# A feed-forward whose seven products run block by block, with sums chained in PSUM

## The reference, cut to what matters

```python
D_FF = 2816
def swiglu(h, w_in, w_out):
    g, u = jnp.split(h @ w_in, 2, axis=-1)
    return (jax.nn.silu(g) * u) @ w_out
# in the first block, after the mixers (x: 1024 x 1024, float32):
x = layer_norm(ALPHA * x + g1 * y, ln1_w, ln1_b)
x = layer_norm(ALPHA * x + g2 * swiglu(x * (1.0 + sc2) + sh2, w_ffn_in, w_ffn_out), ln2_w, ln2_b)
```

## Time and profile before

| | us |
|---|---|
| median of 3 runs | 2177.39 (2175.89 to 2180.31) |
| profiled execution, its own time | 2175.72 |
| its span | 2173.9 |
| feed-forward, first matmul to last | 606.84 to 1313.05 |
| next stage's first matmul | 1329.03 |

### The profile page before, as it was taken

One profiled execution on the slowest core, in us unless ns is written; L12 is line 12 of the kernel. 1 busy time (PEld: TensorE's weight loads), 2 busy tenths in 40 slices (PEclk: granted clock), 3 DMA queues, 4 the chain that ended last, 5 costly groups with the idle time before them and its releaser, 6 DMA issues. The chain is left out here.

```text
span 2173.9 us, 27683 instructions
## 1 busy us (share of the span) xinstructions
PE 2022.9 (93%) x10285; PEld 1510.1 (69%) x10285; DVE 1490.8 (69%) x2639; ACT 804.9 (37%) x1608; POOL 437.0 (20%) x477
## 2 busy tenths in 40 slices
PE   6999999998989999989999995989999888989998
PEld 3844474576877788767877784856888665658876
DVE  6582695568978951795489656479999788761433
ACT  2222112154244532552335323365221346760425
POOL 2910001133310000000000003214667351300110
PEclk8999999999999999999999997999999999999999
DMA  8443120113246422541464533112211002012101
GB/s 322 170 130 117 38 78 1 30 50 145 97 136 184 137 77 76 157 136 52 119 181 134 160 112 120 60 46 72 59 49 48 28 1 78 1 70 106 39 0 78
DMA packets 229530, 200.78 MB, mean 92 GB/s; under 512 B 16062, under 2 KB 199678, under 8 KB 226074
## 3 DMA queue, kind: packets, MB, share of 16 engines
q1 hardware_dynamic: 226426, 188.59, 27.7%
q0 software_dynamic: 2880, 10.49, 1.2%
q10 hardware_dynamic: 96, 0.02, 0.0%
HBM read 185.10 MB, written 12.64 MB: 91 GB/s over the span
## 5 line engine op out<-in xcount | busy, mean ns | idle before, releaser
L1754 PE MATMUL ps<-ff_rh,ff_wh 128*128 128x512 f32 x592 | 232.6, 393 | 20.1 <-DVE ff_wl L2071 19.7
L1756 PE MATMUL ps<-ff_rh,ff_wl 128*128 128x512 f32 x592 | 230.5, 389 | 0.0
L1755 PE MATMUL ps<-ff_rl,ff_wh 128*128 128x512 f32 x592 | 230.4, 389 | 0.0
L2071 DVE TENSOR_TENSOR ff_wl<-ff_wa,ff_wh 128x512 fp32r<-128x512 f32 (+1 forms) x212 | 143.0, 683 | 66.9 <-ACT ff_wh L1957 66.8
L1957 ACT ACTIVATE ff_wh<-ff_wa 128x512 fp32r<-128x512 f32 (+1 forms) x212 | 130.2, 620 | 145.7 <-DMA ff_wa<-in_w_ffn_out 74.4
L2781 DVE TENSOR_SCALAR_CACHE_REDUCE pj_junk<-NM,prm 128x384 uint8<-128x384 f32 (+1 forms) x186 | 163.7, 944 | 1.1
L1754 PE MATMUL ps<-pj_part,h 128*128 128x512 f32 x384 | 153.1, 399 | 0.2 <-ACT PJ L2638 0.2
L1755 PE MATMUL ps<-pj_part,h 128*128 128x512 f32 x384 | 150.3, 391 | 0.0
L1756 PE MATMUL ps<-pj_part,h 128*128 128x512 f32 x384 | 150.2, 391 | 0.0
L1754 PEld LDWEIGHTS ps<-ff_rh,ff_wh 128*128 128x128 f32 x592 | 111.1, 188 | 52.0 <-issue 29.8
L1754 PE MATMUL ps<-ff_h,ff_wh 128*128 128x512 f32 x352 | 137.6, 391 | 5.1 <-DVE ff_wl L2071 2.2
(11 more groups left out here) (625 smaller groups left out, 4421.7 us busy)
## 6 DMA issues: line engine op xcount, KB each, us to landing
ff_wa<-in_w_ffn_in SPq DMA_DIRECT2D x148, 256.0 KB, 2.8
ff_wb<-in_w_ffn_in SPq DMA_DIRECT2D x104, 256.0 KB, 3.2
s_wm<-in_w_mod SPq DMA_DIRECT2D x16, 1024.0 KB, 4.6
pj_raw<-in_w_in SPq DMA_DIRECT2D x64, 256.0 KB, 2.6
ff_wa<-in_w_ffn_out SPq DMA_DIRECT2D x48, 256.0 KB, 2.7
mod_w<-in_w_mod SPq DMA_DIRECT2D x8, 1024.0 KB, 8.6
mod_x<-in_x SPq DMA_DIRECT2D x8, 512.0 KB, 13.4
mx_spread<-mx_lfd SPq DMA_DIRECT2D x16, 256.0 KB, 4.1
```

The source lines that it names most:

```text
L1754: nc.tensor.matmul(out, w[0], x[0], start=first, stop=False)
L1755: nc.tensor.matmul(out, w[0], x[1], start=False, stop=False)
L1756: return nc.tensor.matmul(out, w[1], x[0], start=False, stop=last)
L2071: v.tensor_tensor(l[:, 0:n, :], a[:, 0:n, :], h[:, 0:n, :].bitcast(F32), ALU.subtract).then_inc(lo, 1)
```

## The change

- **Order of the units.** After four blocks of the first two products, the seven products run block by block: products 6, 5, 7, 4, 3 of block f beside products 1 and 2 of block f + 1 (`IN_UNITS`). Product p reads token operand p; all seven are made once, at the start, and kept in SBUF.
- **Chains.** Products 1, 6, 7 and 4 of a block run into one bank, products 5 and 3 into another, 2 into a third. ACT copies the bank after product 1, after 6 and after 7 and PE goes on adding to it; DVE adds products 2, 5 and 3 to the copies. This is another form of the seven-product scheme, with four sums of weight tiles on a block's four tiles, each loaded once (`weight_sums`, `weight_sum4`, on DVE; POOL has none).
- **Hidden tensor.** POOL stores the hidden blocks 0 to 19 in DRAM (`ff_hid`); they are loaded again towards the end, over the token operands and the weights, and split by ACT and DVE. Blocks 20 and 21 stay.
- **Output.** Each hidden block is multiplied into eight banks at once: a first pass with 512 output columns for both token halves (24 matmuls per weight block of 128 x 512), a second and a third with the other 512 columns for one half each (12 matmuls). The weight blocks lie in 5, 3 and 5 slots. `ynT` is written once, by two evictions on ACT and two on DVE at each end of a group of four banks. The transposes back and the norm of the first four token tiles lie beside the third pass, after its blocks 1, 6, 11 and 16.
- The transposes of the last four token tiles use one pair of banks (6, 7) instead of two.

```diff
         pe.wait_ge(g2_ev, 1)
-        if i >= 2:
+        if i > NT // 2:
+            pe.wait_ge(thi, 2 * i)
+        elif i >= 2:
...
+LEAD = 4
+BLOCK = {1: 0, 2: 1, 6: 2, 5: 3, 7: 4, 4: 5, 3: 6}
+PAIRED = (6, 5, 7, 4, 3)
+IN_UNITS = [(p, f) for p in (1, 2) for f in range(LEAD)]
+IN_UNITS += [(p, f + s) for f in range(0, LEAD, 2) for p in PAIRED for s in range(2)]
+IN_UNITS += [(p, LEAD) for p in (1, 2, 6, 5, 7)]
+for _f in range(LEAD, NF - 2):
+    IN_UNITS += [(1, _f + 1), (4, _f), (2, _f + 1), (3, _f), (6, _f + 1), (5, _f + 1), (7, _f + 1)]
+IN_UNITS += [(1, NF - 1), (4, NF - 2), (2, NF - 1), (6, NF - 1), (5, NF - 1), (7, NF - 1), (3, NF - 2), (4, NF - 1), (3, NF - 1)]
+OUT_UNITS = [(g, f) for g in range(3) for f in range(NF)]
+KEPT = 2
...
+    slot_kb = ((4, 6), (0, 2), (164, 166), (168, 170), (8, 10), (24, 26), (32, 34))
...
+    cycles = ((0, 1, 2, 3, 4), (4, 0, 1), (5, 6, 0, 1, 4))
+    slot_of = [cycles[g][f % len(cycles[g])] for g, f in OUT_UNITS]
...
+    hid = nc.dram_tensor("ff_hid", (NS, 2, P, HALF), F32, kind="Internal").ap()
...
+    sums_at.update({at_unit[1, f] - 4: f for f in range(LEAD + 1, NF)})
...
+    sum4_at.update({at_unit[2, f] - 4: f for f in range(LEAD + 1, NF)})
...
+            def pair_load(f):
+                for h in range(2):
+                    sp.dma_start(pair_raw[f % 2][:, h], w1[:, h, :, 1, f * P:(f + 1) * P]).then_inc(main_in[f % 2][2], 16)
+
+            def out_load(q):
+                g, f = OUT_UNITS[q]
+                if last_user(q) >= 0:
+                    sp.wait_ge(om, last_user(q) + 1)
+                elif g == 2:
+                    sp.wait_ge(om, NF + 5 + f + 1)
+                n = slice(0, HALF) if g == 0 else slice(HALF, D)
+                sp.dma_start(out_slots[slot_of[q]][0][:], w2[f][:, n]).then_inc(out_in[slot_of[q]], 16)
...
+            for f in range(2, NF):
+                for j in range(2):
+                    if f - 2 < LEAD:
+                        sp.wait_ge((sm, sm4)[j], (3 * (f - 2) + 3, f - 1)[j])
+                    else:
+                        sp.wait_ge(mm, at_unit[1 + j, f - 2] + 1)
+                    main_load(f, j)
+                sp.wait_ge(mm, at_unit[4, f - 2] + 1)
+                pair_load(f)
...
+            sp.wait_ge(mm, at_unit[2, NF - 1] + 1)
+            for f in range(0, 5):
+                back_load(f)
+            for f, p in ((5, 6), (7, 5), (9, 7)):
+                sp.wait_ge(mm, at_unit[p, NF - 1] + 1)
+                back_load(f)
+                back_load(f + 1)
...
+            for q in range(10, len(OUT_UNITS)):
+                if q == 2 * NF:
+                    sp.wait_ge(om, 2 * NF)
...
                     for r, name in enumerate(("ln2_w", "ln2_b", "norm_mix_2")):
                         sp.dma_start(K.fe_rows[:, r, :], I[name].to_broadcast([P, D])).then_inc(K.fe_rows_in, 16)
                     for i in range(2):
                         sp.dma_start(K.fe_x[i][:], K.x1[i * P:(i + 1) * P, :]).then_inc(K.fe_x_in[i], 16)
...
+                out_load(q)
...
+            for f in range(NS):
+                for t in range(2):
+                    pool.wait_ge((hd0, hd1)[t], f + 1)
+                    sem = lead_st[f - 2] if t == 0 and 2 <= f < LEAD else kept_st[t][f % 2]
+                    pool.dma_start(hid[f, t], place(t, f)[:]).then_inc(sem, 16)
...
+                for n in {5: (), 6: (8,), 7: (9,), 8: (10, 11)}.get(u, (u + 3,)):
+                    if n < NU:
+                        high(n)
...
+                        nc.scalar.activation(place(0, f)[:], a, ACT.Copy).then_inc(s1, 1)
+                    elif p == 6:
+                        stored_wait(act, 1, f)
+                        act.wait_ge(mm, u + 1)
+                        nc.scalar.activation(place(1, f)[:], a, ACT.Copy).then_inc(cu2, 1)
+                    elif p == 7:
+                        if f >= 2:
+                            act.wait_ge(hd1, f - 1)
+                        act.wait_ge(mm, u + 1)
+                        nc.scalar.activation(third[f % 2][:], a, ACT.Copy).then_inc(cu3, 1)
...
+                if u == NI + NF - 1:
+                    act.wait_ge(oh, 1)
+                    for n in (0, 2):
+                        evict(0, n, n)
...
+            def weight_sums(f):
+                r = [t[0] for t in main[f % 2]]
+                dve.wait_ge(main_in[f % 2][2], 32 * loads_before(f))
+                if f >= 2:
+                    dve.wait_ge(mm, at_unit[5, f - 2] + 1)
+                v.tensor_tensor(r[3][:], r[4][:], r[5][:], ALU.add).then_inc(sm, 1)
+                dve.wait_ge(main_in[f % 2][0], 16 * loads_before(f))
+                dve.wait_ge(sm, 3 * f + 1)
+                if f >= 2:
+                    dve.wait_ge(mm, at_unit[6, f - 2] + 1)
+                v.tensor_tensor(r[2][:], r[3][:], r[0][:], ALU.subtract).then_inc(sm, 1)
+                v.tensor_tensor(r[4][:], r[0][:], r[4][:], ALU.subtract).then_inc(sm, 1)
...
+            def crossed(i, before):
+                dve.wait_ge(J.thi, 2 * (4 + i) + 2)
+                dve.wait_ge(xlo, KH)
+                tile_sum(5, 7, 1, i)
+                dve.wait_ge(xs, before + 1)
+                tile_sum(6, 3, 5, i)
+                dve.wait_ge(xlo, 2 * KH)
+                dve.wait_ge(xs, before + 2)
+                tile_sum(4, 2, 6, i)
...
+                    if p == 2:
+                        dve.wait_ge(s1, f + 1)
+                        dve.wait_ge(mm, u + 1)
+                        v.tensor_tensor(place(0, f)[:], place(0, f)[:], K.bank[4 + f % 2][:], ALU.add).then_inc(c11, 1)
+                    elif p == 7:
+                        dve.wait_ge(cu3, f + 1)
+                        v.tensor_tensor(third[f % 2][:], third[f % 2][:], K.bank[6 + f % 2][:], ALU.add).then_inc(c22, 1)
+                    elif p == 4:
+                        dve.wait_ge(sl0, f + 1)
+                        dve.wait_ge(mm, u + 1)
+                        v.tensor_tensor(place(0, f)[:], place(0, f)[:], K.bank[f % 4][:], ALU.mult).then_inc(hd0, 1)
+                    elif p == 3:
+                        dve.wait_ge(cu2, f + 1)
+                        dve.wait_ge(mm, u + 1)
+                        v.tensor_tensor(place(1, f)[:], place(1, f)[:], K.bank[6 + f % 2][:], ALU.add).then_inc(c12, 1)
...
+                elif p == 6:
+                    pe.wait_ge(s1, f + 1)
...
+                elif p == 7:
+                    pe.wait_ge(cu2, f + 1)
+                elif p == 4:
+                    pe.wait_ge(cu3, f + 1)
...
+                    for i, (w, x) in enumerate(((wh, row_high), (wh, row_low), (wl, row_high))):
+                        last = nc.tensor.matmul(K.bank[bank][:], w[:, k, :], x[p][:, k, :], start=(k == 0 and i == 0 and p in (1, 2, 5)),
+                                                stop=(k == KH - 1 and i == 2), skip_group_check=True)
...
+            for q, (g, f) in enumerate(OUT_UNITS):
+                pe.wait_ge(lo, NI + q + 1)
+                r, wh, wl = out_slots[slot_of[q]]
+                for h in range(2):
+                    if g and h != g - 1:
+                        continue
+                    if g == 0:
...
+                    for n in range(4):
+                        bank = 4 * h + n
+                        if f == 0:
+                            if g == 0 and h == 0 and n < 2:
+                                pe.wait_ge(hd0, NS + n + 1)
+                            elif g == 0 and h == 1:
+                                pe.wait_ge((c11, c12)[n // 2], NS + n % 2 + 1)
+                            elif g:
+                                pe.wait_ge((oea, oed)[n % 2], 2 * g - 1 + n // 2)
+                        for i, (w, x) in enumerate(((wh, hid_high), (wh, hid_low), (wl, hid_high))):
+                            last = nc.tensor.matmul(K.bank[bank][:], w[:, n * P:(n + 1) * P], x[f][h][:], start=(f == 0 and i == 0), stop=(f == NF - 1 and i == 2))
+                    if q == NF - 1 and h == 0:
+                        last.then_inc(oh, 1)
+                last.then_inc(om, 1)
+                if g == 2 and f % 5 == 1 and f // 5 < 4:
+                    back(f // 5)
```

More of the change, by code:

```diff
@@ L1777, in stage_join_ffn @@
[L1777 to L1794, removed]
@@ L1819, in stage_join_ffn @@
-    quad_kb = {(0, 0): ((48, 8),), (0, 1): ((72, 4), (96, 4)), (1, 0): ((24, 8),), (1, 1): ((80, 8),)}
-    quad = {q: [K.at(f"ff_q{q[0]}{q[1]}{kb}", kb, [P, n, HALF]) for kb, n in at] for q, at in quad_kb.items()}
-    split_quad = {q: [K.at(f"ff_h{q[0]}{q[1]}{kb}", kb, [P, n, HALF], FR) for kb, n in at] for q, at in quad_kb.items()}
-    def tile(tiles, row, half, f):
-        m = f - next(lo_f for lo_f, hi_f in CHUNKS if lo_f <= f < hi_f)
-        parts = tiles[row, half]
-        return parts[0][:, m, :] if len(parts) == 1 else parts[m // 4][:, m % 4, :]
+    NI = len(IN_UNITS)
@@ new lines, in stage_join_ffn, with place @@
+    third = [K.at(f"ff_u{s}", kb, [P, HALF]) for s, kb in enumerate((18, 74))]
+    def place(half, f):
+        if half:
```

(39 more changed lines are left out.)

658 lines of the change are left out of this document (362 added, 296 removed), and 4 rows, old and new, of the table hid_kb.

## The result

The changed kernel takes 2152.74 us (median of four runs, 2151.52 to 2154.59), the kernel before, beside it, 2177.7: a ratio of 0.9885, 95% interval 0.9868 to 0.9902. The profiled execution took 2153.44 us, its span is 2151.6. The forecast was 2155, from a sum of 2153.2 for the profiled execution.

The account below looks back on a forecast made before the run. PE bounds the kernel, held up now and then by a full DVE. Terms -33.1 + 1.1 + 7 + 15.9 - 14.1 = -23.2, taken as -22.5 from 2175.72: 2153.2 profiled, 2155 us median; range 2143 to 2173.

Parts of the forecast that it names:

- lead: Start of the stage: DVE full, fifteenth product ends at 660.1; +0.6 and +0.5 us for the next pair of blocks.
- 139 products from there: Hidden products after 660.1: 378.2 us plus 0.5, no steady stall.
- first pass: First output pass, 512 columns for both token halves: 119.7 us.
- first seam: Between output passes one and two: PE waits 4.2 us for bank 0, half clock loses 2.8; sum +7, bounds 3 and 8.
- second seam: Between output passes two and three: weights wait behind five loads, +13.0 us, half clock +2.9; sum +16, bounds 9 and 20.
- passes 2 and 3 without the clock's part: Second and third output passes: 59.9 us each, plus 3.2.
- tail: Last matmul to next stage: norm chain and load finish beside the matmuls, 16.4 becomes about 2.3 us, -14.1.
- Steady part: Hidden products block by block: DVE's work per block falls to 9.6 us, no steady stall left, -33.1 us.
- The rival of the late pair of loads: Blocks 5 to 21: weight pair reaches DVE late in every block, 32 us lost in all, 2187 us; chance 0.06.
- The way through DRAM: Hidden blocks, 40 stores by POOL and 40 loads on SP's queue: nothing on the path, 0 us.
- After the stage: Next stage: might gain 1 us from an unbroken clock; taken as 0.
- The runs' median: Whole kernel: median of the runs put 1.7 us above the profiled execution's 2153.2, giving 2155 us.

Follow-up runs that it names:

- the work spread: Changed kernel with ten more DVE instructions of 512 columns in each of blocks 5 to 19, one or two at each product: 2154.25 us, 0.989.
- the same work bunched: Changed kernel with ten more DVE instructions in each of blocks 5 to 19, all at the block's product 6: 2230.59 us, 1.0249.
- the early take: Changed kernel with ACT taking the fifth token tile out of PSUM before waiting for the last norm's variance: 2152.67 us, 0.9878.
- the sums on POOL: Changed kernel with the eight weight sums of the first two blocks on POOL, not DVE: 2158.67 us, 0.992.
- reordering two places: Changed kernel with ACT's evictions ahead of block 24's split and five third-pass weight blocks issued ahead of the row and token tile loads: 2132.22 us, 0.9786.

## Why the prediction was right

The time was forecast 2.3 us too high, and the sum for the profiled execution (2153.2) was 0.2 off; that closeness is partly luck, since the steps missed by up to 2 us in both directions, and the 1.2 us by which the next stage started late came back behind it.

| step | predicted | profile after |
|---|---|---|
| sixteenth product starts (lead) | 660.1 | 661.90 |
| 139 products from there | 378.7 | 380.5 |
| first pass | 119.7 | 119.7 |
| first seam: pause, half clock | 4.2 + 2.8 | 4.1 + 1.4 |
| second seam: pause, half clock | 13.0 + 2.9 | 11.8 + 2.4 |
| passes 2 and 3 without the clock's part | 123.0 | 123.4 |
| tail | 2.3 | 2.7 |
| next stage starts | 1306.7 | 1307.92 |

- *Steady part.* Right, and shown: of the 33 us, 2.4 are left in 139 products, 2.0 of them in three waits. The prediction named bunches beside DVE's share, and the runs tell the two apart: DVE busy 85% of the time, with the work spread, cost nothing, and the same work bunched cost 78 us; shortening DVE's sums in the kernel before took 23 us off it. DVE's old work was read too low, 26 instructions a block for 29; no term of the sum hangs on it. The rival of the late pair of loads did not come about: no wait returns with every block, and six more loads a block changed nothing. The way through DRAM cost nothing either: none of PE's waits is for a hidden tile.
- *The lead.* Its end came 1.8 us late, 0.6 of that with a first product that started later than in the kernel before; this start moves between 605.2 and 608.4 in the runs. The term was built from the wrong pieces: the single pair of banks cost 2.6 us and 1.4 of half clock behind it, not 1.3, and the waits for DVE less than the 7.1 counted (4.9). Since DVE's queue sets the end, the pieces are interchangeable, as the early take showed.
- *The seams.* Both were where and why the prediction put them, and each experiment took away its whole term: 6.0 measured for 5.5 by the trace, 14.3 for 14.2. The clock's part was charged too high, with the 2.9 us lost behind the pause of the earlier trace rows. After 4.1 us of pause, seven matmuls took 3.04 us instead of 1.59; after 11.8 us, eleven took 4.85 instead of 2.49. The Trainium skill's rule in "TensorE: Matmul & The Clock Gate", section "HAM oscillation — how this bites in real kernels", that each such pause is charged half the time spent throttled, agrees with the traces: 1.4 of 3.04, 2.4 of 4.85. That half clock would follow at all was argued from the length of the pause, and length alone does not decide it. The pauses of 1.5 and 1.6 us in the lead (at 638.40 the longer) were followed by 0.23 us a matmul, that of 2.6 us by 0.43; but with the sums on POOL a pause of 3.7 us (626.76 to 630.68) was followed by 0.23 us again, at a granted clock of 1.00. So the clock does not come down with each pause of this length, where the prediction had it do so, and that it did at the first seam was in part luck. What decides it was not tried.
- *The tail.* Right: 16.4 became 2.7, and putting the last norm back to the end gave 9.8 us back.
- *After the stage.* The next stage starts 21.1 us earlier, the span ends 22.3 earlier. The 1.2 us between, taken as 0, lie in the next stage, whose first 37 us ran at 0.77 of the clock instead of 0.73. Why the clock differs there was not tried, and the four runs' spans lie up to 3.1 us apart (2149.7 to 2152.8), so it may be chance.
- *The runs' median* lies 0.7 us below the profiled execution, where the prediction had put it 1.7 above, as it was for the kernel before.

## What to carry to other kernels

An engine that is off the critical path, and busy up to 85% here, stalls PE by where its work stands between two waits and not by how full it is: spread the work over the products before taking any of it away. At every seam of a pass, list what each engine's program does ahead of the instruction that frees a bank or issues the next pass's first loads; reordering two places gave 20.5 us here, beside 25.0 for the whole redesign. When a seam's pause ends, trust the program over the releaser that the row names if two events end within a few tenths of a microsecond.

## What the runs showed of the hardware

DVE and POOL slow each other down when both sum tiles of SBUF: 0.68 us became 1.57 to 1.77 on DVE, and POOL's sums took from 1.30 us, where one began ahead of DVE's instruction, to 1.74, where DVE's was under way. Each of the eight slowed DVE instructions ends 0.54 to 0.56 us behind the POOL sum beside it. The Trainium skill's page "SBUF — State Buffer", section "SBUF: two separate sides", says that a VectorE instruction with two SBUF inputs and a GpSimd instruction that reads SBUF take one pair of ports in turn, each for its whole length; the rows fit that. The kernel before has it too: ahead of its first product a DVE addition that takes 1.23 us in the changed kernel (at 605.49) lay beside one of POOL's sums.

```profile
603.50 1.56 POOL L1923 TENSOR_TENSOR ff_sa<-ff_sa,ff_sb 128x512 f32<-128x512 f32 x1
...
603.95 2.20 DVE L1723 TENSOR_TENSOR jn_h<-jn_h,MOD 128x1024 f32<-128x1024 f32 x1
```

What that cost the kernel before in its lead was not tried.
